# Two transformer stacks on one core: norms turned by token block, the next projection one block ahead, an eight-part weight ring

## The chip, the cores and the metric

One core of one Trainium2 chip runs the whole program. The metric is the device time of one execution in microseconds. TensorE (PE) multiplies, VectorE (DVE), ScalarE (ACT) and GpSimd (POOL) do the rest, and SyncE's queue (SPq) issues the weight loads. All engines run their own instruction streams in order and meet at semaphores.

## The reference

`x` has 256 tokens of 1024 features in float32. The first stack has four layers. Each layer has a mixer (sliding attention with sinks in layers 0 and 3, a gated linear recurrence in layer 1, latent attention in layer 2), cross attention over 256 memory tokens, and a gated feed-forward with a causal three-tap convolution over 2 x 2816 hidden features. After each of the three the tokens are normed:

```python
x = layer_norm(ALPHA * x + y, ln_g[i, 0], ln_b[i, 0])
x = layer_norm(ALPHA * x + memory_cross_attention(x, mem_k, mem_v, x_w_q[i], x_w_o[i]), ln_g[i, 1], ln_b[i, 1])
x = layer_norm(ALPHA * x + conv_glu_ffn(x, f_w_up[i], f_conv_w[i], f_conv_b[i], f_w_down[i]), ln_g[i, 2], ln_b[i, 2])
```

The second stack has two layers that add to the stream instead and norm by root mean square ahead of each part: an attention (with forget gates in layer 0, dilated in layer 1) joined with four heads over a second memory, then a feed-forward of the same size. A last root-mean-square norm gives the output.

## The kernel before

**Weights and precision.** Every matrix product with weights is done in three products of fp32r operands: each float32 is split into a rounded high part and the rest (`hi*hi + lo*hi + hi*lo`, `product`, lines 700 to 702). Weights come in 639 units of 128 x 1024 elements, 512 KB each. SyncE loads a unit into one of `RING` = 6 slots of `w_raw` (`unit_in`, line 525), waiting until the unit six earlier has been subtracted. ScalarE copies it into `w_hi` (`split`, line 1313) once PE has used the unit six earlier, and VectorE subtracts (`w_lo`, line 1728). Both do so at most `AHEAD` = 4 units ahead of the point that their program has reached (`Splitter.units`); `limit` caps this further at the end of a stage.

**Two forms of a projection.** In *feature form* a unit holds 128 output features, the weights are the stationary operand and the 256 tokens move: 24 products of 256 columns. In *token form* the turned tokens `xt` are stationary and 512 weight columns move: 12 products of 512 columns for a unit of two of the eight feature tiles, both token blocks. Feature form gives features on partitions (what a score needs), token form gives tokens on partitions.

**A stage boundary.** `out_finish` (line 1097) makes the second 512 columns of the mixer's or cross attention's output, all eight tiles of token block 0, then of block 1. VectorE adds the stream and takes statistics per block (`norm_part`, lines 2052 to 2058), GpSimd adds epsilon (L2264) and raises to -1/2 (L2266), VectorE scales in two passes (`norm_apply`, lines 2071 and 2074). PE then turns the 128 x 128 tiles of both blocks into banks 4 to 7, two tiles with both blocks to a bank (`turn_blocks`, L768). ScalarE copies each bank to `xt_hi` (L1353) and VectorE subtracts for `xt_lo` (L1743). Since a bank holds both blocks, nothing can be copied before block 1 is turned. The next stage's projection in feature form needs both blocks too. `seed_sums` (L1129) clears four banks with products of zeros for the feed-forward's down sums. The feed-forward (`feed_forward`, line 1132) does one tile of 128 hidden features at a time: two up units, the convolution on ScalarE (L1621) and VectorE (L2143), silu, product, split, and two tiles later one down unit (L1161).

**Order.** Each engine writes its whole program in stages: `program` calls the same steps on all five, and `attend` lays attention groups over one another, with `fill` giving PE projection or output units between groups. Nothing is reordered later.

## Time and profile before

| | us |
|---|---|
| median of 3 runs | 2255.78 (2255.22 to 2257.04) |
| the profiled execution | 2255.68 |
| its span | 2254.4 |
| PE / DVE / ACT / POOL busy | 2100.3 / 1539.6 / 1178.4 / 91.9 |

The clock granted to PE is 0.969 of full speed on average. Times inside the trace are microseconds from the start of the span. A line number names the instruction in the kernel before; `x12` means twelve instructions merged; brackets at the end give how long the engine was idle before and whose result ended that.

### The profile page before, as it was taken

How to read it: one execution, taken by the hardware profiler on the slowest of the kernel's cores; microseconds unless marked ns; L12 is line 12 of the kernel's file. 1: busy time of each engine (PE TensorE's matmuls, PEld its weight loads, DVE VectorE, ACT ScalarE, POOL GpSimd, SP SyncE). 2: the span in 40 equal slices, each digit the busy share in tenths (PEclk: the TensorE clock that was granted, in tenths of full speed). 3: DMA queues.
4: the chain of work that ended last, by engine and by line, in shares of the span. 5: the costliest groups of instructions: out<-in, count | busy, mean ns of one | idle time of the engine just before them, and what ended most of it. 6: DMA issues, size and time to landing. Idle time of an engine off the chain costs nothing.

```text
span 2254.4 us, 34080 instructions
## 1 busy us (share of the span) xinstructions
PE 2100.3 (93%) x13749; PEld 1909.1 (85%) x13749; DVE 1539.6 (68%) x2655; ACT 1178.4 (52%) x2027; POOL 91.9 (4%) x160
## 2 busy tenths in 40 slices
PE   7889999888999989899989999998998999999998
PEld 7778899787799978889977778997977999778997
DVE  4674777786677676577777757777465766666776
ACT  4453555484365555445545535554455555465554
POOL 3000000000000010000000000001000000000000
PEclk9999999998999999999999999999899999999999
DMA  8424666455366554456644437664624665424662
GB/s 279 149 76 136 180 189 189 129 168 168 111 198 179 179 157 121 132 167 186 181 159 134 126 100 222 181 184 126 179 66 140 196 195 179 154 93 136 191 194 87
DMA packets 436205, 356.24 MB, mean 158 GB/s; under 512 B 15858, under 2 KB 381686, under 8 KB 436048
## 3 DMA queue, kind: packets, MB, share of 16 engines
q1 hardware_dynamic: 429296, 332.49, 48.6%
q0 software_dynamic: 6752, 21.57, 2.9%
q8 instruction: 109, 1.79, 0.3%
q14 instruction: 48, 0.39, 0.1%
HBM read 352.97 MB, written 1.05 MB: 157 GB/s over the span
## 4 chain that ended last, share of the span: by engine, by line
PE 83%; DVE 9%; ACT 4%; issue 1%; POOL 1%; DMA 1%; SPq 0%; DVEq 0%; ACTq 0%
PE psum L700 20%; PE psum L702 20%; PE psum L701 20%; PE psum L1161 14%; PE psum L1057 3%; DVE w_lo L1728 1%; PE psum L1043 1%; PE psum L987 1%; DVE xt_lo L1743 1%; DVE x_tok L2074 1%; PE psum L826 1%; DMA tok<-in_mem_dram 1%; ACT w_hi L1313 1%; DVE n_tok L2052 1%; DVE small L2055 1%
## 5 line engine op out<-in xcount | busy, mean ns | idle before, releaser
L1728 DVE TENSOR_TENSOR w_lo<-w_raw,w_hi 128x1024 fp32r<-128x1024 f32 x639 | 752.3, 1223 | 158.8 <-ACT w_hi L1313 157.0
L700 PE MATMUL psum<-xt_hi,w_hi 128*128 128x256 f32 x2744 | 791.6, 288 | 23.1 <-DVE w_lo L1728 15.5
L701 PE MATMUL psum<-xt_lo,w_hi 128*128 128x256 f32 x2744 | 787.2, 287 | 0.0
L702 PE MATMUL psum<-xt_hi,w_lo 128*128 128x256 f32 x2744 | 786.7, 287 | 0.0
L1313 ACT CAST w_hi<-w_raw 128x1024 fp32r<-128x1024 f32 x639 | 646.9, 1048 | 84.5 <-PE psum L702 61.4
L700 PEld LDWEIGHTS psum<-xt_hi,w_hi 128*128 128x128 f32 x2744 | 537.8, 196 | 31.3 <-DVE xt_lo L1743 8.9
L701 PEld LDWEIGHTS psum<-xt_lo,w_hi 128*128 128x128 f32 x2744 | 537.8, 196 | 4.7
L702 PEld LDWEIGHTS psum<-xt_hi,w_lo 128*128 128x128 f32 x2744 | 537.1, 196 | 0.0
L2143 DVE SCALAR_TENSOR_TENSOR qt<-psum,par,qt 128x255 f32<-128x255 f32 (+1 forms) x528 | 217.9, 475 | 163.1 <-ACT qt L1621 162.9
L700 PE MATMUL psum<-w_hi,xt_hi 128*128 128x512 f32 (+4 forms) x700 | 261.8, 374 | 23.8 <-DVE xt_lo L1743 22.5
L702 PE MATMUL psum<-w_hi,xt_lo 128*128 128x512 f32 (+4 forms) x700 | 255.4, 365 | 0.0
L701 PE MATMUL psum<-w_lo,xt_hi 128*128 128x512 f32 (+4 forms) x700 | 255.2, 365 | 0.0
L1621 ACT ACTIVATE qt<-psum,par 128x256 f32<-128x256 f32 x264 | 134.5, 560 | 210.6 <-PE psum L702 210.6
L1161 PE MATMUL psum<-w_hi,hid_hi 128*128 128x512 f32 x528 | 207.8, 394 | 4.8 <-DVE hid_lo L2155 4.8
L1161 PE MATMUL psum<-w_lo,hid_hi 128*128 128x512 f32 x528 | 207.0, 392 | 0.0
L1161 PE MATMUL psum<-w_hi,hid_lo 128*128 128x512 f32 x528 | 205.6, 389 | 0.0
L700 PEld LDWEIGHTS psum<-w_hi,xt_hi 128*128 128x128 f32 x700 | 137.3, 196 | 48.5 <-issue 15.2
L702 PEld LDWEIGHTS psum<-w_hi,xt_lo 128*128 128x128 f32 x700 | 136.9, 196 | 19.9
L701 PEld LDWEIGHTS psum<-w_lo,xt_hi 128*128 128x128 f32 x700 | 137.4, 196 | 17.9
L1626 ACT ACTIVATE kt<-qt 128x256 f32<-128x256 f32 x132 | 55.1, 418 | 181.8 <-DVE qt L2143 181.7
L1353 ACT CAST xt_hi<-psum 128x512 fp32r<-128x512 f32 x78 | 40.9, 591 | 185.5 <-PE psum L768 185.5
L1743 DVE TENSOR_TENSOR xt_lo<-psum,xt_hi 128x512 fp32r<-128x512 f32 (+1 forms) x130 | 75.8, 617 | 67.8 <-ACT xt_hi L1539 39.2
(216 smaller groups left out, 1907.1 us busy)
## 6 DMA issues: line engine op xcount, KB each, us to landing
w_raw<-in_f_w_up_dram SPq DMA_DIRECT2D x176, 512.0 KB, 4.9
w_raw<-in_f_w_down_dram SPq DMA_DIRECT2D x88, 512.0 KB, 5.1
w_raw<-in_w_up_dram SPq DMA_DIRECT2D x88, 512.0 KB, 4.9
w_raw<-in_w_down_dram SPq DMA_DIRECT2D x44, 512.0 KB, 5.0
w_raw<-in_x_w_q_dram SPq DMA_DIRECT2D x32, 512.0 KB, 4.5
w_raw<-in_x_w_o_dram SPq DMA_DIRECT2D x32, 512.0 KB, 4.7
w_raw<-in_a_w_qkv_dram SPq DMA_DIRECT2D x24, 512.0 KB, 4.4
w_raw<-in_w_in_fox_dram SPq DMA_DIRECT2D x20, 512.0 KB, 4.7
```

The costliest lines, as they stand in the source:

```text
L700: self.eng.matmul(out, stat[0], mov[0], start=first, stop=False)
L701: self.eng.matmul(out, stat[0], mov[1], start=False, stop=False)
L702: return self.eng.matmul(out, stat[1], mov[0], start=False, stop=last)
L1057: ins = self.eng.matmul(m.psum[p0:p0 + wide, k, slot * SEQ + q0:(slot + 1) * SEQ], vals(c), m.pt[:, group.g % 2, i, cols], start=c == 0, s ...
L1161: ins = self.eng.matmul(m.psum[:, b + 2 * c, :], stat[x], unit[y][:, 0, cs], start=False, stop=last and x == 1, skip_group_check=True)
L1313: self.up(self.eng.copy(self.m.hi[:, s, :], self.m.raw[:, s, :]), "w_hi", u)
L1353: self.up(self.eng.copy(dst[0][:, j:j + nt, :], self.m.pair(4 + j // 2)[:, 0:nt, :]), "x_hi", self.tag, after, j)
L1621: ins = self.eng.activation(m.qt[:, 2 * s + half, :], out[half], ACT.Identity, scale=col((TAPS - 1) * 2 * FT + half * FT + q), bias=col(TA ...
L1626: self.up(self.eng.activation(m.kt[:, s, :], m.qt[:, 2 * s + silu_half, :], ACT.Silu), "silu", self.tag, q)
L1728: self.up(self.eng.tensor_tensor(self.m.lo[:, s, :], self.m.raw[:, s, :], self.m.hi[:, s, :].bitcast(F32), ALU.subtract), "w_lo", u)
L1743: n = self.up(self.eng.tensor_tensor(dst, src, hi.bitcast(F32), ALU.subtract), "ready", (tag, what), j)
L2143: ins = self.eng.scalar_tensor_tensor(cv[:, d:SEQ], out[half][:, 0:SEQ - d], col((TAPS - 1 - d) * 2 * FT + half * FT + q), cv[:, d:SEQ], A ...
```

## The change

- `RING` becomes 8 for the split parts `w_hi`, `w_lo`, and a new `RAW` = 4 is the number of raw slots. The freed memory also takes in `swap`, which now lies in the second half of `n_tok`'s block 1, and `zeros` goes away.
- `turn_half` turns four tiles of one token block into one bank (banks 4, 5 for block 0 and 0, 2 for block 1 at norms), and `split_half` copies and subtracts that bank alone. `operand` waits for the block that it reads.
- `out_finish` turns the first half of block 0 ahead of the last unit of block 1's products, the second half behind it, and leaves block 1's two turns in `rest`.
- `project_blocks` begins the next stage in token form: block 0 through four units, with the turns of `rest` behind its third and fourth unit, then block 1 through the same four. It makes the sliding queries' first half (now ahead of the keys), the latent keys, the first 512 of 1024 queries of cross attention and the first four feature tiles of the feed-forward. For the last two the tokens are copied to `n_tok` (`keep_first`) and turned to features by PE (`cross_queries`, `up_tile` for q below 2). The recurrence turns block 1 at once (`turn_now`).
- Cross attention's third and fourth query pair change places: the third stands around the turns, the fourth in step 0 of the attention.
- The norm's epsilon is added on VectorE (in `norm_part`, and in `rms_factor` by one instruction), and GpSimd is left with the power. Where the mean of squares comes from ScalarE, both operations stay on GpSimd.
- The down sums start with `start=True` at the first down unit instead of on zeros.
- The order on VectorE is changed: block 0 is scaled ahead of block 1's part, also at the end of a feed-forward.

The diff, cut:

```diff
+RAW = 4
+RING = 8
...
+def turn_bank(key, b, h):
+    return (4, 5, 6, 7)[2 * b + h] if key[0] == "start" or key[1] == "mem" else (4, 5, 0, 2)[2 * b + h]
...
-        s, k, n = u % RING, src.shape[1], src.shape[-1]
-        if u >= RING:
-            self.wait_ge("w_lo", u - RING)
+        s, k, n = u % RAW, src.shape[1], src.shape[-1]
+        if u >= RAW:
+            self.wait_ge("w_lo", u - RAW)
...
+        halves = w.rearrange("(k p) (h n) -> p k h n", p=P, h=2)
+        for j in range(0, KT, 2):
+            self.unit_in(halves[:, j:j + 2, :, 0:2 * P])
+        for m in range(2, FT + 2):
             if m < FT:
                 for half in range(2):
                     c = (half * FT + m) * P
                     self.unit_in(up[:, :, c:c + P])
-            if m >= 2:
-                self.unit_in(down[:, m - 2:m - 1, :])
+            self.unit_in(down[:, m - 2:m - 1, :])
...
+    def token_products(self, k, n, b, u, unit):
+        hi, lo = unit
+        kn = hi.shape[1]
+        for i in range(kn):
+            j = u * kn + i
+            ins = self.product(self.m.psum[:, k, 0:n], self.operand(j, slice(b * P, (b + 1) * P)),
+                               (hi[:, i, :], lo[:, i, :]), j == 0, j == KT - 1)
+        return ins
+    def project_blocks(self, what, ks, n, by="kept"):
+        units = []
+        for k in ks:
+            self.claim(k)
+        for u in range(KT // 2):
+            units.append(self.take(2, n))
+            ins = self.token_products(ks[0], n, 0, u, units[u])
+            if u == KT // 2 - 1:
+                self.up(ins, "made", self.tag, what, 0)
+            if u >= KT // 2 - 2 and self.rest:
+                self.rest.pop(0)()
+        for u, unit in enumerate(units):
+            ins = self.token_products(ks[1], n, 1, u, unit)
+            self.used(ins, "made", self.tag, what)
+        self.call("w_used", self.made["w_used"], "made", self.tag, what, 1)
+        for b, k in enumerate(ks):
+            self.free[k] = (by, self.tag, what, b)
+    def turn_half(self, key, b, h):
+        src = self.m.x_tok if key[1] == "norm" or key[0] == "first" else self.m.n_tok if key[1] == "applied" else self.m.tok
+        k = turn_bank(key, b, h)
+        if key[1] is not None:
+            self.wait_ge("normed", *key, b, h)
+        self.claim(k)
+        for a in range(HALF):
+            j = h * HALF + a
+            ins = self.eng.transpose(self.m.quad(k)[:, a, :], src[:, b, j * P:(j + 1) * P], self.m.ident[:])
+        self.up(ins, "turned", key, b, h)
+        self.free[k] = ("ready", key, "bank", b, h)
...
+    def turn_rest(self, key):
+        self.rest = [lambda: self.turn_half(key, 1, 0), lambda: self.turn_half(key, 1, 1)]
+        self.x = key
+    def turn_now(self):
+        while self.rest:
+            self.rest.pop(0)()
...
+    def cross_queries(self):
+        m = self.m
+        for j in range(2):
+            k = (4, 6)[j]
+            self.claim(k)
+            for b in range(TB):
+                self.wait_ge("kept", self.tag, "first", b)
+                for a in range(2):
+                    c = (2 * j + a) * P
+                    ins = self.eng.transpose(m.pair(k)[:, a, b * P:(b + 1) * P], m.n_tok[:, b, c:c + P], m.ident[:])
+            self.up(ins, "made", self.tag, "q", j)
+            self.free[k] = ("kept", self.tag, "q", j)
...
-    def out_finish(self, part):
+    def out_finish(self, part, scale, key):
 
         for b in range(TB):
             self.claim(b + 2)
-        units = [self.take(2, BANK) for _ in range(KT // 2)]
-        for b in range(TB):
-            for k in range(KT):
-                hi, lo = units[k // 2]
+        units = []
+        def products(b, j):
+            hi, lo = units[j]
+            for k in (2 * j, 2 * j + 1):
                 ins = self.product(self.m.psum[:, b + 2, :], self.out_tile(k, slice(b * P, (b + 1) * P)),
                                    (hi[:, k % 2, :], lo[:, k % 2, :]), k == 0, k == KT - 1)
-                if b == TB - 1 and k % 2 == 1:
-                    self.used(ins, "summed", self.tag, 1, 1)
-            if b == 0:
-                self.up(ins, "summed", self.tag, 0, 1)
+            return ins
+        for j in range(KT // 2):
+            units.append(self.take(2, BANK))
+            ins = products(0, j)
+        self.up(ins, "summed", self.tag, 0, 1)
+        for j in range(KT // 2):
+            if j == KT // 2 - 1:
+                self.turn_half(key, 0, 0)
+            self.used(products(1, j), "summed", self.tag, 1, 1)
         self.summed()
+        self.turn_half(key, 0, 1)
+        self.turn_rest(key)
...
+                if q >= 2:
+                    self.used(self.feature_out(out, self.take(KT, P)), "made", self.tag, q)
+                    continue
+                for b in range(TB):
+                    self.wait_ge("kept", self.tag, "first", b)
+                    c = (2 * half + q) * P
+                    ins = self.eng.transpose(out[:, b * P:(b + 1) * P], m.n_tok[:, b, c:c + P], m.ident[:])
+                if half == 1:
+                    self.up(ins, "made", self.tag, q)
+            self.free[k] = ("conv", self.tag, q)
...
+    def keep_first(self):
+        for b in range(TB):
+            self.units(2)
+            self.wait_ge("made", self.tag, "first", b)
+            self.keep([(self.m.n_tok[:, b, 0:BANK], self.m.psum[:, 6 + b, :])], "first", b)
...
+        part(0, 1)
+        scale(0)
+        self.split_half(key, 0, 0)
+        part(1, 1)
+        self.split_half(key, 0, 1)
+        scale(1)
+        for h in range(2):
+            self.split_half(key, 1, h)
+    def sums_to(self, part, scale, key):
+        for c in range(2):
+            part(0, c)
+        scale(0)
+        if key is not None:
+            self.split_half(key, 0, 0)
+        for c in range(2):
+            part(1, c)
+        if key is not None:
+            self.split_half(key, 0, 1)
+        scale(1)
+        if key is not None:
+            for h in range(2):
+                self.split_half(key, 1, h)
...
+            self.after(self.step(self.eng.bn_aggr(m.norm[:, 2 * b:2 * b + 2], stats[:, b, :])))
+            var = m.norm[:, 2 * b + 1:2 * b + 2]
+            self.up(self.eng.tensor_scalar(var, var, LN_EPS, None, ALU.add), "var", self.tag, b)
...
+        self.up(self.eng.scalar_tensor_tensor(part[0], part[0], RMS_EPS, part[1], ALU.add, ALU.add),
+                "var", self.tag, "x", b)
...
+    def power(self, r, mean, *which):
+        self.up(self.eng.tensor_tensor(r, mean, self.m.neg_half[:, 0:r.shape[1]], ALU.pow), "rstd", *which)
+    def power_of_squares(self, r, mean, *which):
+        self.wait_ge("squared", *which)
+        self.up(self.eng.tensor_scalar(r, mean, RMS_EPS, None, ALU.add), "pool", *which)
         self.wait_ge("pool", *which)
-        self.up(self.eng.tensor_tensor(r, r, self.m.neg_half[:, 0:r.shape[1]], ALU.pow), "rstd", *which)
+        self.power(r, r, *which)
```


## Rows read from the trace of the kernel before

**Rows 1.** The page, section 1: busy time, share and instructions of PE.
```profile
PE 2100.3 (93%) x13749; PEld 1909.1 (85%) x13749; DVE 1539.6 (68%) x2655; ACT 1178.4 (52%) x2027; POOL 91.9 (4%) x160
```
**Rows 2.** The view of waits, PE: us in total, times, longest us.
```profile
PE psum L768 <- DVE x_tok L2074: 47.9, 28, 3.5
PE psum L700 <- DVE xt_lo L1743: 29.5, 23, 8.9
```
**Rows 3.** Stretches: length, busy time per engine, PEclk, DMA share, GB/s.
```profile
157.64:164.08 6.44, 2.64 (x17) 2.00 (x16) 5.51 (x10) 1.11 (x3) 1.87 (x3) 0.85 0.00 0
164.08:168.92 4.84, 4.84 (x24) 4.84 (x23) 4.49 (x6) 4.82 (x6) 0.65 (x2) 0.50 0.62 223
229.80:236.75 6.95, 4.46 (x22) 2.90 (x20) 5.91 (x10) 1.63 (x4) 2.38 (x4) 0.79 0.00 1
426.62:437.81 11.19, 3.73 (x17) 2.54 (x17) 10.07 (x17) 1.11 (x3) 2.65 (x5) 0.73 0.04 14
1282.17:1284.90 2.73, 2.73 (x14) 2.73 (x14) 2.58 (x4) 2.73 (x5) 0.71 (x2) 0.50 0.65 170
```
**Rows 4.** The chain that ended last, first down products of two tiles in ffn0.
```profile
255.99 2.75 PE psum L1161 x12
264.49 2.75 PE psum L1161 x12
```
**Rows 5.** Timeline of the boundary mix0 to cross0: start, us, engine, line.
```profile
149.61 2.34 DVE L1728 TENSOR_TENSOR w_lo<-w_raw,w_hi 128x1024 fp32r<-128x1024 f32 x2
152.40 0.69 DVE L2052 SCALAR_TENSOR_TENSOR n_tok<-x_tok,psum 128x512 f32<-128x512 f32 x1 [0.45 <-PE psum L702]
153.85 0.21 DVE L2058 BATCH_NORM_AGGREGATE norm<-small 128x2 f32<-128x12 f32 x1
154.09 0.75 DVE L2071 SCALAR_TENSOR_TENSOR n_tok<-n_tok,norm,gain_row 128x512 f32<-128x512 f32 x1
154.15 0.77 POOL L2264 TENSOR_SCALAR norm<-norm 128x1 f32<-128x1 f32 x1 [124.56 <-DVE norm L2058]
155.01 0.57 POOL L2266 TENSOR_TENSOR norm<-norm,neg_half 128x1 f32<-128x1 f32 x1
157.06 0.75 DVE L2074 SCALAR_TENSOR_TENSOR x_tok<-n_tok,norm,bias_row 128x512 f32<-128x512 f32 x1
157.64 1.03 PE L768 MATMUL psum<-ident,x_tok 128*128 128x128 f32 x8
```
**Rows 6.** Timeline behind ffn0, GpSimd.
```profile
427.52 0.22 POOL L2264 TENSOR_SCALAR norm<-norm 128x1 f32<-128x1 f32 x1 [190.66 <-DVE norm L2058]
```
**Rows 7.** Timeline, PE: two waits, in ffn3 and ahead of second0.
```profile
1365.10 0.58 PE L700 MATMUL psum<-xt_hi,w_hi 128*128 128x256 f32 x1 [3.86 <-DVE w_lo L1728]
1570.75 0.66 PE L768 MATMUL psum<-ident,n_tok 128*128 128x128 f32 x2 [5.84 <-ACT mem_kt L1319]
```
**Rows 8.** Timeline, ScalarE: copies of turned keys and queries in mix3.
```profile
1201.85 2.60 ACT L1319 COPY kt<-psum 64x256 f32<-64x256 f32 x8 [4.83 <-PE psum L784]
1208.52 1.11 ACT L1321 ACTIVATE qt<-psum 128x512 f32<-128x512 f32 x2
```
**Rows 9.** A steady feed-forward: a load's issue, the casts (timeline), landings of 260 to 400.
```profile
304.44 0.37 SPq L525 DMA_DIRECT2D w_raw<-in_f_w_up_dram  x1
310.61 3.14 ACT L1313 CAST w_hi<-w_raw 128x1024 fp32r<-128x1024 f32 x3
DMA to landing us min/median/max: 3.4/5.2/7.2
```
**Rows 10.** Stretches behind two waits of PE, columns as in rows 3.
```profile
483.70:488.00 4.30, 4.30 (x36) 4.30 (x37) 3.35 (x3) 4.25 (x10) 1.37 (x1) 1.00 0.68 235
1228.14:1232.00 3.86, 3.86 (x14) 2.66 (x16) 2.26 (x13) 1.96 (x9) 0.00 (x0) 0.50 0.01 2
```
**Rows 11.** Timeline, PE: these two waits.
```profile
483.70 0.36 PE L700 MATMUL psum<-xt_hi,w_hi 128*128 128x256 f32 x1 [2.31 <-DVE w_lo L1728]
1228.14 1.23 PE L826 MATMUL psum<-kt,qt 128*128 128x128 f32 x3 [3.07 <-DVE stat L1991]
```

More of the change, by code:

```diff
@@ L761, in turn_blocks @@
             for j in range(tiles):
                 k = 4 + j // 2
-                if after is not None and j % 4 == 0:
-                    self.wait_ge("normed", self.tag, after, b, j // 4)
                 if j % 2 == 0 and b == 0:
@@ L890, in latent_start @@
                 self.turn_latent()
[L891 removed]
+            unit = self.take(2, C_QR)
             for b in range(TB):
[L893 to L896 removed]
+                ins = self.token_products(ks[b], C_QR, b, u, unit)
             self.used(ins, "made", self.tag, "cq")
@@ L1160, in down_part @@
             for x, y in ((0, 0), (0, 1), (1, 0)):
-                ins = self.eng.matmul(m.psum[:, b + 2 * c, :], stat[x], unit[y][:, 0, cs], start=False,
-                                      stop=last and x == 1, skip_group_check=True)
+                ins = self.eng.matmul(m.psum[:, b + 2 * c, :], stat[x], unit[y][:, 0, cs],
+                                      start=first and x == y == 0, stop=last and x == 1)
             return ins
+        self.project_blocks("first", (6, 7), BANK)
         for q in range(FT):
@@ L1570, in sum_unit, with out_finish @@
             self.units()
-    def out_finish(self, part):
+    def out_finish(self, part, scale, key):
         self.limit = self.unit + RING - 1
@@ L1638, in feed_forward, with sums_to @@
         self.limit = None
-    def sums_to(self, part):
+    def sums_to(self, part, scale, key):
         for b in range(TB):
@@ L1743, in low, with split_banks @@
         n = self.up(self.eng.tensor_tensor(dst, src, hi.bitcast(F32), ALU.subtract), "ready", (tag, what), j)
-        for a in range(1, nt):
+        for a in range(nt):
             self.call("ready", n, "ready", (tag, what), j + a)
+            for b in range(TB):
+                self.call("ready", n, "ready", (tag, what), j + a, b)
         self.call("ready", n, "ready", tag, what, j)
-    def split_banks(self, after, dst, tiles=KT):
+    def split_banks(self, after, dst, tiles):
         hi, lo = dst
@@ L1755, in split_banks, with split_half, split_turned @@
         self.call("ready", self.made["ready"], "ready", (self.tag, after), "hid")
+    def split_half(self, key, b, h):
+        hi, lo = (x[:, h * HALF:(h + 1) * HALF, b * P:(b + 1) * P] for x in self.m.xt)
+        self.wait_ge("x_hi", key, b, h)
+        n = self.up(self.eng.tensor_tensor(lo, self.m.quad(turn_bank(key, b, h)), hi.bitcast(F32), ALU.subtract),
+                    "ready", key, "bank", b, h)
+        for j in range(h * HALF, (h + 1) * HALF):
+            self.call("ready", n, "ready", key, j, b)
+    def split_turned(self, key):
+        for b in range(TB):
+            for h in range(2):
+                self.split_half(key, b, h)
+    norm_to_features = split_turned
     def start(self):
         self.eng = self.nc.vector
-        self.n_read = None
         self.e_read = [None, None]
-        self.step(self.eng.memset(self.m.zeros[:].bitcast(F32), 0.0), "zeros")
     def memory_keys_values(self):
-        self.split_banks(None, self.m.xt)
+        self.split_turned(("start", None))
         self.units(KT + KT)
@@ L2026, in sum_unit, with out_finish @@
             self.units()
-    def out_finish(self, part):
+    def out_finish(self, part, scale, key):
         self.limit = self.unit + RING - 1
@@ L2115, in add_part @@
         self.up(self.eng.tensor_tensor(h, h, m.psum[:, b + 2 * c, :], ALU.add), "added", self.tag, b, c)
-        if c == 1:
-            self.rms_factor(b)
-    def norm_to_features(self):
-        self.rms_apply(1)
-        for b in range(TB):
-            for c in range(2):
-                self.counts[("normed", self.tag, "norm", b, c)] = self.counts[("normed", self.factor, "applied", b, c)]
-        self.n_read = ("turned", self.tag, "norm", KT - 2)
-        self.split_banks("norm", self.m.xt)
     def feed_forward(self, params, silu_half):
@@ L2233, in memory_queries @@
         self.units(2)
-    def end(self):
-        self.rms_apply(1)
 class Pool(Engine):
@@ L2300, in stream_power, with sums_to @@
         m = self.m
-        self.power(m.norm[:, 20 + b:21 + b], m.norm[:, 16 + 2 * b:17 + 2 * b], RMS_EPS, "var", self.tag, "x", b)
-    def out_finish(self, part):
+        self.wait_ge("var", self.tag, "x", b)
+        self.power(m.norm[:, 20 + b:21 + b], m.norm[:, 16 + 2 * b:17 + 2 * b], self.tag, "x", b)
+    def sums_to(self, part, scale, key):
         for b in range(TB):
             part(b, 1)
-    def sums_to(self, part):
-        for b in range(TB):
-            for c in range(2):
-                part(b, c)
+    out_finish = sums_to
     def sliding_start(self, j):
```

340 lines of the change are left out of this document (148 added, 192 removed).

## The prediction

> **What bounds the kernel now.** I read the page's busy times first: PE is busy 2100.3 us of 2254.4 [rows 1]. So a change counts only through PE's idle time, its number of columns or its clock. Next I asked what PE waited for [rows 2]. The largest entry is the turning of the normed tokens (L768, 47.9 us), then the low halves of the turned tokens (L700 on L1743, 29.5 us). Both lie mostly at the stage boundaries. Stretches cut there [rows 3] show 6.44 us without a product between the output products and the next projection (157.64 to 164.08), 6.95 after cross attention and 11.19 after the feed-forward. All twelve gaps together, read the same way, are about 125 us, the 16 turns of each among them. Behind the gap the granted clock is 0.50 (1.2 GHz) for 4.84 us; at the last boundary of that kind it is so for 2.73 us. Half of that is lost: 2.4 to 1.4 us, together some 20 us.
>
> Rates: one feed-forward tile repeats every 8.50 us, and its 12 products of 512 columns take 2.75 [rows 4], 0.227 us each; the other 48, of 256 columns, then take 0.120 each. Eight turns show 1.03 us, of which the last one's end is drain: 0.9.
>
> **The change, one boundary worked through (mix0 to cross0).** Before, block 0 is complete at 152.40, the last product ends at 157.64 where the turns begin (call it E), the next starts at 164.08 [rows 3, 5]. Afterwards:
>
> The ring of 8 lets VectorE subtract four units ahead of block 0's norm instead of two. They start at 149.61 and cost 1.17 us each [rows 5], so the norm starts at 154.3, 1.9 us late. Add and statistics take 1.45 us (152.40 to 153.85), the aggregate 0.24, the new epsilon step as much: L2071 starts at 156.2. The Pool operation that goes away looks like 0.77 us, but the same operation takes 0.22 at 427.52, where VectorE is not in L2071 [rows 6]. In rows 5 it ends just behind L2071. So what is on Pool beside L2071 ends behind it, and now that is the power itself. Its bounds are 0.57 (not held) and 1.4 (held through L2071's 0.75, then 0.09 and 0.57). I take 1.4, as the nearest row is held: L2074 at 157.7, first half of block 0 at 158.4, second at 159.9. Against the old order the chain from Z (block 0 summed) to its end is 5.6 us, before 5.4 (157.06 + 0.75 - 152.40): the epsilon step gains nothing.
>
> The Trainium skill, SBUF — State Buffer, section Who interferes with whom, says that a VectorE instruction with two SBUF inputs contends with a GpSimd instruction that reads SBUF, and the second to issue waits. By that rule the trace agrees (0.77 beside L2071, 0.22 beside L2052, which reads one operand from PSUM), and the power would be held as I took it; without it all eight attention boundaries would give 0.65 us more, 5 us in all.
>
> PE reaches the first turn after 18 of block 1's 24 products, 152.20 + 4.08 = 156.3, waits 2.1 us there, turns (0.45), does the six last products (1.36, to 160.3), turns again; the low half is ready by 160.5 behind scale(0). First product of cross0: 160.7, not 164.08, and without half clock. Block 0's 24 products (5.44) then cover block 1's norm: its statistics end at 162.5, turned values at 164.7 and 166.2, where PE arrives at 164.8 and 166.7; with 8 turns (0.9) and block 1 (5.44) the four units are done at 172.5, E + 14.9. Before, they were at 178.0, E + 20.4 (6.44 + 96 x 0.120 + half clock + the last drain). Gain 5.5. Back go 8 turns of the query tokens (0.9), covered for their copies by cross_query(2, 0), and 0.3 because step 1 of the attention has lost its fill. That is 4.2 at cross0, and up to 1 us less where the old half clock was shorter: 3.65 mean, four times, **14.6**.
>
> **The others.** Cross to feed-forward: old 6.95 + 11.52 + 1.35 = 19.8; new 14.9 + 0.9 of turns + 0.65 for the copy of block 1 that nothing covers = 16.5. Three times 3.3: **9.9**. The zero products (four, inside the 6.95) lay in a wait; removing them is nothing.
> The two feed-forwards with the second memory's norm stop at 1365.10 and, alike, at 1732.42 [rows 7], because the squares and the 2.48 us of L1916 stand ahead of the splits. Now keep_first stands behind them too. I get E + 22 for the work that was done at E + 26: **4.0** at ffn3, **2.5** at gated0, whose memory load is issued 2 us later.
> Feed-forward to mixer: VectorE is the bound (10.07 of 11.19 us busy). First products start 4.7 + 0.65 us behind E instead of 11.2, but stop again for block 0's second half. Latent **+2.4** (its normed compressed keys also wait for a row load), sliding3 **+1.0** (the sink load, issued behind the norm, holds the splits, and q0's rotation holds its turn by 1.6), recurrent **-1.6**, since it turns everything first and pays the 0.24, the 0.65 and part(1, 0) earlier.
> Sliding now turns the keys last. Eight key copies take 2.60 us, two query copies 1.11 [rows 8]: scores start 1.9 later. In sliding3 it is in the sum already; mix0 has no gain against it: **-1.9**.
> Second stack: at 1570.75 PE waited 5.84 us for a key copy in the bank to be turned into [rows 7]; banks 0 and 2 relieve half: **+2.5**. Then **+1.0** (second1), **+1.6** (gated1: old 5.9 + 11.5, no half clock). Tail: rms_apply(0) now ahead of part(1, *): **-0.4**.
>
> **Raw units, 6 to 4.** In a steady tile the three loads are issued from 304.44, 1.14 us apart, and the casts start at 310.61 [rows 9]. With 4 slots these are units S+1 to S+3, S+1 cast at 311.66: 7.2 us after issue; landings there are 3.4/5.2/7.2. So nothing in most tiles; bounds 0 and about 1 us in a tile whose casts come late, and ScalarE's idle of 1.78 in a tile absorbs that. I take 0. Block products in tokens need 0.17 us less per unit, which is in the 5.44s.
>
> Sum: 14.6 + 9.9 + 6.5 + 1.8 - 1.9 + 5.1 - 0.4 = **35.6 us**. The profiled execution took 2255.68 us (span 2254.4), the median is 2255.78; 2255.7 - 35.6 = **2220**.
>
> **Rivals.**
> A, more: Pool isn't held beside L2071 and the loads for the third and fourth early split don't delay anything, the 2.1 us wait shrinks to 0.6 at eleven boundaries: 12 to 16 us more, **2206**. For it: only tiny operands; against it, rows 5 and 6.
> B, half clock stays: the wait at the turn, a further wait behind it and turns between make the clock fall again. A wait of 2.31 us left it at 1.00, one of 3.07 was followed by 0.50 [rows 10, 11]; mine is 2.1, between nothing and 3. If it falls at most boundaries, 11 x 1.8 = 20 us come back: **2240**.
> C, slower: four raw slots become the bound in the 132 feed-forward tiles. One mechanism, at L525: a load is issued only when the unit four before is subtracted. It decides from 35.6 / 132 = 0.27 us a tile; at 0.5 us a tile, about what a landing of 7.2 plus a late cast leaves, 66 us are added: **2286**. Against: PE uses a unit a whole tile after its subtraction.
> D, the change doesn't do what it says: one VectorE does both blocks in order, so block 0's lead is eaten by the early splits, scale(0) and copies, and only retransposition remains: within a few us of before, **2253**. Against: VectorE is busy 5.51 of the 6.44 us, and block 1's part of it now lies under products.
>
> **Chances.** Forecast 0.60 (own range 2212 to 2230), A 0.13, B 0.17, C 0.06, D 0.04. About 0.2% (4.5 us) is what can be told from no change. Faster: forecast, A and B, 0.90 and a little of D, 0.91; same 0.03; slower 0.06. Range 2205 to 2243: all of the forecast, most of A and B; C, D and the tails of A and B are out.
>
> **What would show it.** Right: no stretch without products longer than 3 us between output products and next projection; waits at L768 for x_tok near 2 us a boundary, 25 us in all; Pool's power about 1.3 us beside L2071; clock 1.00 across attention boundaries; the recurrent gap not shorter; kt copies last ahead of the first scores in sliding. Wrong: ScalarE's w_hi waiting for w_raw loads inside the feed-forward, tiles of more than 8.50 us, 0.50 behind attention boundaries, or a gap in step 1 of cross attention above 1 us. More than 50 us gained would mean that I misread what the wait for block 0 costs.

## The result, and the profile after

The changed kernel takes 2240.1 us (2239.5 to 2242.1, 4 runs) against 2256.4 (2255.2 to 2257.6, 4 runs) on the same chip: a ratio of 0.9928, 95% interval 0.9914 to 0.9942. It is faster, inside my range, but the gain is 16.3 us where I forecast 35.6. The number lies on that of rival B, but not by B's mechanism, as the runs show. The time of the profiled span is 2239.0 us (2254.4 before).

First the page of the changed kernel, its busy times, to be set against [rows 1]:

```profile
PE 2085.5 (93%) x13325; PEld 1876.8 (84%) x13325; DVE 1544.3 (69%) x2678; ACT 1179.8 (53%) x2047; POOL 73.5 (3%) x126
```

PE is busy 14.8 us less, and that is nearly the whole 15.4 by which the span shrank. Its waits did not shrink: those of 0.3 us and more, added up over the trace, are 143.7 us before and 143.3 after. They moved. The waits of PE in the changed kernel (instruction, what it waited for, us in total, times, longest), to be set against [rows 2]:

```profile
PE psum L814 <- DVE x_tok L2195: 26.7, 16, 4.8
PE psum L720 <- DVE qt L2247: 18.4, 6, 5.6
PE psum L720 <- DVE xt_lo L1835: 17.2, 10, 7.4
PE psum L1221 <- ACT n_tok L1391: 12.1, 8, 5.7
PE psum L895 <- ACT kt L1391: 4.7, 2, 2.3
```

The first row is the old L768, down from 47.9 to 26.7 (I had written 25). The second and fourth did not exist before. L2247 is VectorE's convolution of a feed-forward tile, and a product at L720 waits for it six times, once in each feed-forward: 2.36 us four times, 5.60 and 3.32 us in ffn3 and gated0, where the second memory's norm stands in VectorE's queue ahead of it. L1221 turns the first tiles' products back to features.

To place the gain I cut each trace at VectorE's first addition of a stage's sums (L2052 and L2115 before, L2173 and L2231 after); a stage's length is the distance between two such starts, so it begins inside the boundary ahead of it. Two pairs of these rows as an example, first of the kernel before:

```profile
219.11 0.69 DVE L2052 SCALAR_TENSOR_TENSOR n_tok<-x_tok,psum 128x512 f32<-128x512 f32 x1 [1.69 <-PE psum L702]
424.46 0.68 DVE L2052 SCALAR_TENSOR_TENSOR n_tok<-x_tok,psum 128x512 f32<-128x512 f32 x1
```

and of the changed one:

```profile
216.38 0.69 DVE L2173 SCALAR_TENSOR_TENSOR n_tok<-x_tok,psum 128x512 f32<-128x512 f32 x1 [1.67 <-PE psum L722]
421.80 0.68 DVE L2173 SCALAR_TENSOR_TENSOR n_tok<-x_tok,psum 128x512 f32<-128x512 f32 x1
```

So the stage ffn0 took 205.35 us before and 205.42 after. All stages, in us, as the difference from the kernel before (negative is a gain), beside the forecast; e1, e3 and f1 are experiments below:

| stage | before | forecast | changed | e3 features | e1 four banks | f1 |
|---|---|---|---|---|---|---|
| cross0, 1, 2, 3 | 72.2, 71.9, 71.2, 71.3 | -3.65 each | -4.8, -4.6, -3.9, -3.9 | -4.8, -4.6, -3.8, -3.9 | -4.4, -4.6, -3.8, -3.6 | -4.8, -4.6, -3.8, -3.6 |
| ffn0, 1, 2 | 205.4, 205.1, 204.9 | -3.3 each | +0.1, +0.4, +1.6 | +1.9, +2.2, +2.4 | -4.4, -4.1, -3.9 | -4.1, -3.8, -3.6 |
| ffn3, gated0 | 217.8, 218.1 | -4.0, -2.5 | -0.9, +2.7 | -4.7, -0.7 | -6.2, -3.0 | -10.7, -11.3 |
| gated1 | 201.0 | -1.6 | +2.3 | +4.0 | -1.8 | -1.8 |
| mix1, 2, 3 | 98.6, 93.1, 96.0 | +1.6, -2.4, -1.0 | +1.6, -2.4, -0.6 | +2.1, -2.6, -2.4 | +2.0, +1.4, +0.1 | +1.8, -1.8, -1.3 |
| second0, 1 | 148.4, 120.7 | -2.5, -1.0 | -1.7, -3.2 | -1.8, -3.1 | -1.8, -3.1 | -3.3, -3.1 |

Not every stage can be read so finely. mix0 ended at 146.96, 149.07 and 151.34 in three executions of which the last two are of the same code up to there. Over the traces of all versions whose code doesn't differ there, mix2 and second0 spread over some 4 us, mix3 and ffn3 over about 2, and ffn2 took 206.5 us in the changed kernel and 204.1 in e4. Most of the others repeat to some 0.4 us. What can be read: the attention boundaries gained what was forecast and a little more, and all six feed-forwards fell short, by 3.4, 3.7, 4.9, 3.1, 5.2 and 3.9 us: 24 us together.

What happens at their head, in the timeline of the changed kernel at ffn0 (start, us, engine; in brackets the idle time before it and what ended it):

```profile
241.84 0.59 ACT L1391 COPY n_tok<-psum 128x512 f32<-128x512 f32 x1 [0.61 <-PE psum L722]
242.48 0.98 PE L1221 MATMUL psum<-ident,n_tok 128*128 128x128 f32 x7 [0.57 <-ACT n_tok L1391]
243.06 1.02 ACT L1713 ACTIVATE qt<-psum,par 128x256 f32<-128x256 f32 x2 [0.64 <-PE psum L1221]
244.12 1.65 DVE L2247 SCALAR_TENSOR_TENSOR qt<-psum,par,qt 128x255 f32<-128x255 f32 x4 [1.44 <-ACT qt L1713]
245.82 0.39 PE L720 MATMUL psum<-xt_hi,w_hi 128*128 128x256 f32 x1 [2.36 <-DVE qt L2247]
```

The product at 245.82 is the first of tile 2. up_tile claims bank[q % 2], and tile 2's bank 4 is tile 0's, which the convolution reads until 245.77. Before the change the two up units of tile 1 (48 x 0.120 = 5.8 us) stood between tile 0's products and this claim. The same convolution in the kernel before:

```profile
245.57 1.65 DVE L2143 SCALAR_TENSOR_TENSOR qt<-psum,par,qt 128x255 f32<-128x255 f32 x4 [2.69 <-ACT qt L1621]
```

It ended at 247.22, and tile 2's first product came at 250.07. Now tiles 0 and 1 together are eight turns, and the last seven of them take 0.98 us. Behind the wait the clock falls (columns: stretch, its length, busy time and count of PE, PEld, DVE, ACT, POOL, granted clock, DMA share, GB/s):

```profile
245.82:250.82 5.00, 5.00 (x29) 5.00 (x30) 3.35 (x8) 2.67 (x7) 0.00 (x0) 0.66 0.41 120
```

A clock of 0.66 over 5 us is a mean of the two levels, 1.2 and 2.4 GHz; 1.7 us are lost in it. In the attention boundary it stays up, where [rows 3] had 0.50 for 4.84 us, and the first turns wait 1.28 us behind mixers and 1.59 behind cross attention; over the 13 to 16 us from the first turn it is 1.00 at all eight. Windows of the changed kernel at mix0 to cross0, from the first turn:

```profile
159.83:162.50 2.67, 2.67 (x16) 2.32 (x17) 2.55 (x4) 0.74 (x2) 0.00 (x0) 1.00 0.72 191
162.50:173.00 10.50, 10.50 (x52) 8.68 (x51) 8.64 (x14) 5.29 (x8) 1.69 (x3) 1.00 0.29 106
```

### The profile page after: what moved, and what is told of

It is laid out like the page before. It is cut to its first block, busy times and chain, and to the rows that moved or that the text cites. A ratio compares the mean times of both kernels' runs of the same rounds, so it can differ in the third digit from the quotient of the medians.

```text
span 2239.0 us, 33115 instructions
## 1 busy us (share of the span) xinstructions
PE 2085.5 (93%) x13325; PEld 1876.8 (84%) x13325; DVE 1544.3 (69%) x2678; ACT 1179.8 (53%) x2047; POOL 73.5 (3%) x126
## 3 DMA queue, kind: packets, MB, share of 16 engines
q8 instruction: 105, 1.72, 0.3%
## 4 chain that ended last, share of the span: by engine, by line
PE 79%; DVE 14%; ACT 4%; DMA 2%; issue 1%; POOL 1%; SPq 0%; DVEq 0%; ACTq 0%
PE psum L720 18%; PE psum L722 18%; PE psum L721 18%; PE psum L1230 15%; DVE w_lo L1820 4%; PE psum L1125 3%; PE psum L1111 1%; DVE small L2176 1%; DVE n_tok L2173 1%; PE psum L814 1%; PE psum L895 1%; PE psum L1054 1%; DMA tok<-in_mem_dram 1%; DVE qt L2247 1%; DVE x_tok L2195 1%
## 5 line engine op out<-in xcount | busy, mean ns | idle before, releaser
L720 PE MATMUL psum<-xt_hi,w_hi 128*128 128x256 f32 x2424 | 696.1, 287 | 29.4 <-DVE qt L2247 18.4
L721 PE MATMUL psum<-xt_lo,w_hi 128*128 128x256 f32 x2424 | 693.6, 286 | 0.0
L722 PE MATMUL psum<-xt_hi,w_lo 128*128 128x256 f32 x2424 | 693.3, 286 | 0.0
L720 PEld LDWEIGHTS psum<-xt_hi,w_hi 128*128 128x128 f32 x2424 | 472.3, 195 | 37.5 <-DVE qt L2247 20.1
L721 PEld LDWEIGHTS psum<-xt_lo,w_hi 128*128 128x128 f32 x2424 | 472.3, 195 | 4.8
L722 PEld LDWEIGHTS psum<-xt_hi,w_lo 128*128 128x128 f32 x2424 | 472.3, 195 | 0.0
L720 PE MATMUL psum<-w_hi,xt_hi 128*128 128x512 f32 (+4 forms) x860 | 328.8, 382 | 24.1 <-DVE xt_lo L1835 17.2
L2247 DVE SCALAR_TENSOR_TENSOR qt<-psum,par,qt 128x255 f32<-128x255 f32 (+1 forms) x528 | 218.1, 476 | 170.0 <-ACT qt L1713 170.0
L722 PE MATMUL psum<-w_hi,xt_lo 128*128 128x512 f32 (+4 forms) x860 | 318.4, 370 | 0.0
L721 PE MATMUL psum<-w_lo,xt_hi 128*128 128x512 f32 (+4 forms) x860 | 318.3, 370 | 0.0
L720 PEld LDWEIGHTS psum<-w_hi,xt_hi 128*128 128x128 f32 x860 | 167.2, 194 | 54.1 <-issue 16.2
L1230 PEld LDWEIGHTS psum<-w_hi,hid_hi 128*128 128x128 f32 x528 | 99.7, 189 | 24.6 <-DVE hid_lo L2259 7.3
```

The lines of the kernel that those rows point to most:

```text
L720: self.eng.matmul(out, stat[0], mov[0], start=first, stop=False)
L721: self.eng.matmul(out, stat[0], mov[1], start=False, stop=False)
L722: return self.eng.matmul(out, stat[1], mov[0], start=False, stop=last)
L1230: ins = self.eng.matmul(m.psum[:, b + 2 * c, :], stat[x], unit[y][:, 0, cs], start=first and x == y == 0, stop=last and x == 1)
L2247: ins = self.eng.scalar_tensor_tensor(cv[:, d:SEQ], out[half][:, 0:SEQ - d], col((TAPS - 1 - d) * 2 * FT + half * FT + q), cv[:, d:SEQ], A ...
```

## The experiments

My theory after the two traces: the forecast's mechanism works at every boundary, but the token form of the feed-forward's first tiles has taken away what covered tile 0's convolution, and bank 4 is not free. Rivals: tile 0's chain bounds the first down product anyway; the clock takes the gain; the token form is worth the forecast and the loss is in the tiles (four raw units); VectorE's early splits hold the norm. Each ratio below is taken against the kernel before on the same chip (its medians there are 2257.6 to 2258.6 us), so ratios compare between experiments better than times do. In the cuts of code, `...` marks what is left out.

**e1, four banks.** Tile q uses a bank of four in turn, in the three engines:

```
-        bank = (4, 6)
+        bank = (4, 6, 5, 7)
...
-            k = bank[q % 2]
+            k = bank[q % 4]
...
```

> Changed kernel, feed-forward tiles rotate over banks 4, 6, 5, 7 instead of 4, 6. Bank theory: in the changed kernel the gain of the new norm is given back behind the 8 re-turns, where tile 2 claims bank 4 while tile 0's convolution still reads it (L720 on qt L2247: 2.36 us four times, 3.32 and 5.60 once, 18.4 in all) and where the granted clock then falls to 0.50 (another 1.5 to 2.4 us each). With a free bank both go: 18 + 6 x 1.5 = 27 us less than the changed kernel's 2240, so about 2213 to 2220. Chain theory: the wait only changes its name, since the first down product needs tile 0's hid anyway and the second unit of tile 3 is subtracted only behind tile 1's convolution; then the waits move to L1230 on hid_lo or to L720 on w_lo and less than 5 us are won: 2235 to 2240. Clock theory: the wait goes but the clock still falls behind the boundary, 18 us less minus the half clock that stays: 2222 to 2226.

Measured: 2215.7 us, ratio 0.9814 (0.980 to 0.9828). The bank theory gave 2213 to 2220. The same place in e1's timeline:

```profile
244.82 0.98 PE L1221 MATMUL psum<-ident,n_tok 128*128 128x128 f32 x7 [0.57 <-ACT n_tok L1391]
245.40 1.02 ACT L1713 ACTIVATE qt<-psum,par 128x256 f32<-128x256 f32 x2 [0.64 <-PE psum L1221]
245.56 0.36 PE L720 MATMUL psum<-xt_hi,w_hi 128*128 128x256 f32 x1
246.46 1.65 DVE L2247 SCALAR_TENSOR_TENSOR qt<-psum,par,qt 128x255 f32<-128x255 f32 x4 [1.44 <-ACT qt L1713]
```

Tile 2's first product now has no wait and starts 0.9 us ahead of the convolution, and the stretch behind it, in e1's windows, is at full clock:

```profile
245.56:250.56 5.00, 5.00 (x45) 5.00 (x44) 3.03 (x8) 3.89 (x7) 0.00 (x0) 1.00 0.93 284
```

45 products in 5 us against 29. The wait on qt is gone from e1's list and none took its place, which falsifies the chain theory; the clock went with the wait, so it was no cause of its own. The six feed-forwards gain 29.5 us between them against the changed kernel; some 7 us of it went back in this execution in mix0, mix2 and mix3, stages that don't repeat. This is the cause of the miss, shown.

**e2, tile 2's first unit ahead of the re-turns** (on top of e1), to cover the copy at L1391:

```
...
+        up_tile(2, (0,))
+        up_tile(0)
+        up_tile(1)
+        up_tile(2, (1,))
...
```

> As e1_four_banks, and tile 2's first up unit is multiplied ahead of the 8 re-turns, its second behind them, so that ScalarE's copy of the first products (L1391, 12.1 us of waits at L1221, up to 5.7) lies beneath 2.9 us of products. Bank theory with this cover: another 4 x 0.57 plus most of 2.0 and 2.9 of the 7.6 us of the two stages with a memory norm, so 5 to 8 us less than e1_four_banks. Rival: tile 0's chain (base, convolution, silu, product, split, some 6.5 us) starts 2.9 us later and the first down product waits for it: no gain over e1_four_banks, within 2 us, and a new wait of 1 to 3 us at L1230 on hid_lo in each of the six feed-forwards.

Measured: 2221.5 us, ratio 0.9841 (0.9828 to 0.9855), 6 us slower than e1. The rival's direction held, its place only in part. PE's waits in e2:

```profile
PE psum L720 <- DVE w_lo L1826: 20.7, 5, 8.4
PE psum L1231 <- DVE hid_lo L2265: 10.9, 12, 1.0
```

The down products wait longer than in e1 (10.9 us in all against 4.8), 1.01 us more in each of the six feed-forwards, as the rival said. The waits for the copy, 11.0 us in e1, are gone. But w_lo takes 20.7 us where e1 had 8.5, and the growth lies in the two feed-forwards with the second memory's norm alone: 4.8 us at ffn3 and 8.4 at gated0, against 1.4 and none. At ffn3 VectorE scales the memory's tokens and clears mem_kt (1334.15 to 1338.97) before it subtracts the units that PE now wants sooner. It was VectorE's queue that I should have looked at.

**e3, the feed-forward's tiles 0 and 1 in features again**, two units each, all else as in the changed kernel:

```
...
-        self.project_blocks("first", (6, 7), BANK)
+        self.turn_now()
...
```

> Changed kernel, but the feed-forward's tiles 0 and 1 are projected in features again as before (units of 8 x 128 rows, no copy, no re-turns, and all four halves of the norm turned before the first product); the norm by blocks, the token form in cross attention and all else stay. Theory (the token form gives the feed-forward nothing in this form, because it lays bare tile 0's convolution): within 5 us of the changed kernel, 2235 to 2245. Rival (the token form is worth the 3.3 to 4 us a stage that I forecast, and the loss is somewhere else, in the tiles themselves): 6 x 3.5 = 21 us slower than the changed kernel, about 2260.

Measured: 2241.4 us, ratio 0.9931 (0.9916 to 0.9946), no difference from the changed kernel: in the form in which it was put in, the token form gave the feed-forwards nothing in all. By the table it wins 0.8 to 1.9 us in each of the four feed-forwards without a memory norm, 6.3 together, and loses 3.8 and 3.4 in ffn3 and gated0; with the bank free (e1) the same form is 6.3 us better than features in ffn0.

**e4, epsilon back on Pool**, ahead of the power.

```
+            self.up(self.eng.tensor_scalar(r, self.m.norm[:, 2 * b + 1:2 * b + 2], LN_EPS, None, ALU.add),
+                    "pool", self.tag, "eps", b)
```

> Changed kernel with the epsilon step back on Pool ahead of the power; the turns and all else stay. My forecast's step: the epsilon step on VectorE gains nothing, as the power is held beside L2192 anyway: then 2240 within 2 us. Rival (no hold: the power alone is done 0.5 to 0.8 us sooner at each of the eleven norms, and the wait at the first turn, 1.3 to 1.6 us, shows it): this kernel is 5 to 8 us slower than the changed one, 2245 to 2248. In the trace: Pool's power beside L2192 about 1.1 us and the first turn's wait the same (first case), or a wait at L814 longer by 0.5 or more (second).

Measured: 2242.6 us, ratio 0.9931 (0.9919 to 0.9944): not to be told from the changed kernel. The cross stages are longer by 0.4 to 0.5 us each, 1.8 us in all, and the first turns wait 1.72 us at the attention boundaries, where the changed kernel has 1.28 and 1.59. So the step does cost something on Pool, but the rival's 5 to 8 us don't show. Pool in the changed kernel at cross0's norm, then beside it the same operation at mix0's:

```profile
225.44 0.75 DVE L2192 SCALAR_TENSOR_TENSOR n_tok<-n_tok,norm,gain_row 128x512 f32<-128x512 f32 x1
225.49 1.12 POOL L2365 TENSOR_TENSOR norm<-norm,neg_half 128x1 f32<-128x1 f32 x1 [56.74 <-DVE norm L2181]
...
158.13 0.78 DVE L2192 SCALAR_TENSOR_TENSOR n_tok<-n_tok,norm,gain_row 128x512 f32<-128x512 f32 x1
158.18 0.57 POOL L2365 TENSOR_TENSOR norm<-norm,neg_half 128x1 f32<-128x1 f32 x1 [128.93 <-DVE norm L2181]
```

The power is held to 1.12 us at block 0 of the four cross norms and takes 0.55 to 0.57 at block 0 of the other eight of the first stack, where L2192 takes 0.77 or 0.78 instead of 0.75. In e4 the added step of 0.78 is held at block 0 each time and the power behind it (0.57) never.

**f1, the second memory's norm behind tile 8** instead of ahead of tile 0 (on top of e1):

```
...
+            if q == 8 and self.memory is not None:
+                self.memory_norm_now(self.memory)
...
```

> On top of e1_four_banks: the second memory's norm on ScalarE and VectorE is issued behind tile 8 of the feed-forward instead of ahead of its first tile. Theory (queue order: in ffn3 and gated0 ScalarE's two squares stand ahead of the copy of the first products, and VectorE's L2023 ahead of its splits): the waits at L1221 of 2.04 in ffn3 and 4.45 and 2.04 in gated0 fall to 0.57 or less, the 1.41 at L720 on w_lo goes, and the half clock behind them (1.11 and 1.31 by my count) too: 8 to 11 us less than e1_four_banks, 2205 to 2208. Rival: 3.5 us of work in the middle of a tile stretches the tiles there, since ScalarE and VectorE lie ahead of PE by less than that: 3 to 5 us come back at L1230 on hid_lo or L720 on w_lo, so 2209 to 2213.

Measured: 2201.8 us, ratio 0.9748 (0.9733 to 0.9762), 14 us less than e1 and more than either theory gave. What I had not seen is in e1's timeline at gated0:

```profile
1698.56 1.06 ACT L1568 ACTIVATE e<-tok 128x1024 f32<-128x1024 f32 x1 [4.69 <-DMA tok<-in_mem_dram]
...
1702.53 0.57 ACT L1391 COPY n_tok<-psum 128x512 f32<-128x512 f32 x1
1703.16 0.33 PE L1221 MATMUL psum<-ident,n_tok 128*128 128x128 f32 x1 [4.45 <-ACT n_tok L1391]
```

ScalarE stood 4.69 us for the load of the memory itself, with the copy that PE needed queued behind. In f1 there is no such wait. The kernel before has it too: there ScalarE's first square at gated0 (L1477) waits 5.93 us for the same load.

**h1, the kernel before with that move alone:**

> The kernel before the change, with the second memory's norm alone issued behind tile 8 of the feed-forward. It tells how much of the 14 us that this brought on top of e1_four_banks belongs to the changed kernel's copy of the first products (a copy the kernel before doesn't have). If the copy queued behind the squares is what cost it: the kernel before wins only its two waits of 3.9 us on w_lo and a part of the half clock behind them, 5 to 8 us, 2248 to 2252. If the norm's place costs the same in any form: 12 to 14 us, 2243.

Measured: 2243.1 us, ratio 0.9935 (0.9922 to 0.9948). So the second answer: the norm's place cost the kernel before as much (6.5 us in ffn3 and 6.2 in gated0 by the cut above), and this one move is worth as much as the whole change.

**f3, two of the four early splits behind the first turned half** (on top of e1), and **g2, one of the four** (on top of f1; `+ 6` for `+ 5`):

```
+        self.limit = self.unit + 5
         self.units(KT // 2)
         self.limit = None
         part(0, 1)
         scale(0)
         self.split_half(key, 0, 0)
+        self.units(0, more=True)
```

> On top of e1_four_banks: at the attention boundaries VectorE subtracts two units ahead of block 0's norm as before the change, and the other two behind the first turned half of block 0. Theory (the four early splits delay block 0's norm): the norm starts up to 2.4 us earlier, PE's wait at the first turn (1.27 to 1.6 us at ten boundaries) falls to 0 to 0.3, 8 to 12 us less than e1_four_banks: 2204 to 2208. Rival (the two splits moved behind scale(0) are needed as soon): the next projection's third unit, or block 0's second turned half and block 1's part, come 2.4 us later, and waits of 0.5 to 2 us at L720 on w_lo or at L814 on x_tok take their place: 0 to 6 us gained or lost, 2210 to 2220.

> On top of f1_memory_norm_late: three units subtracted ahead of block 0's norm at the attention boundaries, one behind the first turned half (f3 had two and two, and was 5 us slower than e1_four_banks). If the order of VectorE is a trade that has its best point between, the first turn's wait falls from 1.3 to 1.6 us to about 0.3 and xt_lo comes 1.2 us later, where f3 paid 15.2 us at L720 on L1855 over some eight boundaries: within 3 us of f1_memory_norm_late, 2199 to 2205. If each split behind the turn costs what it saves in front or more: 2 to 4 us slower.

Measured: f3 2220.8 us, ratio 0.9833 (0.9816 to 0.985); g2 2198.5 us, ratio 0.9738 (0.9725 to 0.9752). f3's waits show the trade:

```profile
PE psum L720 <- DVE xt_lo L1855: 22.7, 15, 2.5
PE psum L814 <- DVE x_tok L2197: 15.4, 8, 4.7
```

L814 falls by 12 us and L1855 rises by 15; as a whole f3 and e1 overlap in their intervals. One unit behind looks like the better point: the cross stages are 0.4 to 0.7 us shorter than f1's and ffn0 to ffn3 0.8, though as a whole g2 and f1 overlap in their intervals. g2 is the fastest version: 2.6% under the kernel before, 1.9% under the changed one.

**f4, three raw units** (`RAW = 3`, on top of e1), and **j1, six raw units and a ring of seven** (on top of g2):

> On top of e1_four_banks: three raw units instead of four. It tells whether the raw slots bound the tiles (rival C of the prediction) and how far off they are. If four were just enough, three make ScalarE's cast wait for a landing of 5.4 us in every feed-forward tile: at 0.5 to 1.5 us a tile 66 to 200 us more, 2280 or above. If the loads have slack (a unit is used a whole tile after its subtraction), nothing in the tiles and 5 to 15 us at the stage heads: 2220 to 2230.

> On top of g2_three_splits_early: six raw units and a ring of seven parts, where the changed kernel has four and eight (the same memory); the eighth unit is cast and subtracted behind block 0's first turned half. It asks what four raw units cost. In the changed kernel ScalarE waits about 70 us for w_raw landings where the kernel before waited 12, and at mix0 the four early subtractions start at 154.0 and not at 149.6 as I forecast, because casts wait 0.9 and 1.6 us for landings. If that is on the path, six slots let them start 2 to 4 us sooner: each of the eight attention boundaries 0.5 to 1.5 us shorter, 4 to 12 us less, 2187 to 2195. Rival: the landings are hidden (VectorE waits for block 0's sums anyway), and the ring of seven holds one unit back at each projection in blocks: within 3 us or up to 10 us slower, 2196 to 2208.

Measured: f4 2318.8 us, ratio 1.0264 (1.0239 to 1.0289); j1 2200.2 us, ratio 0.974 (0.9726 to 0.9753). With three units a tile still takes 8.50 us, so both my pictures of f4 were wrong: the cost is as high as in the first and the place that of the second. Each cross stage is 5 us longer, each feed-forward 6.5 to 15, all at their heads, as f4's waits say:

```profile
PE psum L814 <- DVE x_tok L2195: 48.1, 17, 5.2
PE psum L1221 <- ACT n_tok L1391: 38.0, 7, 13.3
```

j1 does away with ScalarE's waits for landings (all w_raw rows together 69.8 us in the changed kernel, 13.1 in j1) and gains nothing. They were hidden at mix0 too, against what I wrote ahead of j1. VectorE's first addition and its early splits, in the kernel before (the splits are in [rows 5], at 149.61) and in the changed one:

```profile
146.96 0.69 DVE L2052 SCALAR_TENSOR_TENSOR n_tok<-x_tok,psum 128x512 f32<-128x512 f32 x1 [1.70 <-PE psum L702]
...
149.07 0.69 DVE L2173 SCALAR_TENSOR_TENSOR n_tok<-x_tok,psum 128x512 f32<-128x512 f32 x1 [1.70 <-PE psum L722]
151.72 4.62 DVE L1820 TENSOR_TENSOR w_lo<-w_raw,w_hi 128x1024 fp32r<-128x1024 f32 x4
```

The splits start 2.65 us behind the first addition in both, and in j1 as well (151.52 and 154.17), with no wait ahead of them; the whole boundary lies later. Four is enough, three is not: rival C was one slot away, at the stage heads and not in the tiles.

**f5 and g1, a filler for PE at the three feed-forward to mixer boundaries**, 24 products on top of e1, then 6 on top of f1:

```
...
+            for _ in range(FILL):
+                ins = self.eng.matmul(self.m.psum[:, 7, 0:SEQ], self.m.mem_v[:, 0, 0:P], self.m.mem_v[:, 0, 0:SEQ],
+                                      start=True, stop=True)
...
```

> On top of e1_four_banks: at the three feed-forward to mixer boundaries PE runs 24 products of 256 columns into a bank that nobody reads (about 2.7 us of extra work, not part of the computation) behind the last down product, where it otherwise waits 2.90 us for block 0's norm. Clock theory: the granted clock falls to 0.50 there because PE stands still, so with the filler it stays at 1.00 behind the first turns; the half clock's cost of 0.74 to 0.93 at ffn0 and ffn1 and 2.0 at ffn2 goes: 3 to 5 us less than e1_four_banks in these stages. Rival: the later wait of 4.83 us (mix1) and of 3.17 (mix2) make it fall anyway and the filler delays the first turn by up to 0.3 us: within 1 us of e1_four_banks.

> On top of f1_memory_norm_late: the filler of f5_fill_24 with 6 products instead of 24 (they took 10.4 us for 24, 0.43 us each, so 6 take 2.6 us, against a wait of 2.6 to 2.9 us; they are not part of the computation). Clock theory: at ffn0, ffn1 and ffn2 the granted clock stays at 1.00 over the first turns and first products, 0.7 to 2 us less each: 2 to 4 us less than f1_memory_norm_late, 2198 to 2200. Rival: the wait for block 1 (4.8 us in mix1) makes the clock fall there all the same and the others are too small: within 1.5 us of it.

Measured: f5 2237.6 us, ratio 0.9903 (0.9886 to 0.9919); g1 2200.6 us, ratio 0.9751 (0.9737 to 0.9765). f5 was mis-sized and doesn't tell what the clock is worth; its filler in the timeline:

```profile
422.18 10.52 PE L1201 MATMUL psum<-mem_v 128*128 128x256 f32 x48
```

24 products in 10.5 us, 7.6 more than the wait of 2.9 that they were to fill. The three mixer stages are 7.2, 4.0 and 5.3 us longer than e1's, most of the 22 us by which f5 is slower. With six the clock stays up at ffn2's boundary. The 8 us from its first turn, f1 and then g1:

```profile
1153.86:1161.86 8.00, 7.62 (x25) 5.82 (x26) 7.34 (x13) 1.17 (x2) 0.55 (x1) 0.62 0.01 2
```

```profile
1151.26:1159.26 8.00, 6.50 (x33) 4.77 (x33) 7.68 (x14) 1.23 (x3) 0.54 (x1) 1.00 0.00 0
```

At 0.62 PE is busy 7.62 us with 25 instructions, at 1.00 it is busy 6.50 with 33: it waits for VectorE instead. At ffn1's boundary the same stretch goes from 0.79 to 0.96, at ffn0's from 0.58 to 0.89. But there PE waits 5.14 us for block 1 next, and behind that wait g1 shows

```profile
431.76:437.00 5.24, 4.86 (x20) 4.09 (x21) 3.25 (x8) 3.19 (x5) 1.10 (x2) 0.50 0.41 122
```

as g1's rival said. The three mixers are 1.2, 0.7 and 0.6 us shorter; the last two are less than mix2 and mix3 spread by themselves, and the whole can't be told from f1. VectorE is busy 7.68 of the 8 us there, so a faster PE mostly waits.

## Why the prediction was wrong, step by step

- **What bounds the kernel, attention boundaries (14.6):** right. The four cross stages gain 17.2 us. Counted from the first addition, block 0's sums are added 1.7 us later than before, where I had put 1.9 for the two more splits. The first turn waits 1.28 us behind mixers, where I had 2.1, since the power isn't held there, and 1.59 behind cross attention, where it is.
- **"Cross to feed-forward ... Three times 3.3: 9.9", ffn3 4.0, gated0 2.5, gated1 1.6:** this is the step that failed. I worked out when block 0's and block 1's products are done and added "0.9 of turns + 0.65 for the copy", and took for granted that the work of tile 2 follows. I counted what the re-turns cost and not what the products they replace had covered. The bank of tile 0 was not in my list of resources, though L2247 reads it and the claim is in the code. In ffn0 the claim costs 2.36 us of waiting and 1.7 of half clock, against a shortfall of 3.4. Measured: -2.0, +0.9, -2.7 and -2.3 us of gain in the place of 9.9, 4.0, 2.5 and 1.6. With the bank freed the same terms are 12.4, 6.2, 3.0 and 1.8 (e1), so the rest of the boundary was worth at least what I had, and e1 ends at 2215.7, where I had 2220. My 9.9 also took 1.35 us of old half clock; the kernel before lost 2.0 at ffn0 (0.50 from 236.75 to 240.70), so that term was small by 0.6 there.
- **Mixers (latent +2.4, sliding3 +1.0, recurrent -1.6):** the numbers are 2.4, 0.6 and -1.6. Only the recurrent one repeats (1.5 to 2.1 us longer in the changed kernel, e1, e3, e4 and f1). For the other two the agreement may be luck: mix2 runs from 2.6 us shorter to 1.4 longer in the same five, mix3 from 2.4 shorter to 0.1 longer. The kt copies come last ahead of sliding's scores and PE waits 2.35 us for them. mix0 can't be read, so its -1.9 is neither shown nor refuted.
- **Second stack, second0 +2.5, second1 +1.0:** 1.7 and 3.2, and second0 took 145.0 us in f1 and 149.1 in g1, whose code is the same there, so its 1.7 can't be told from 2.5. At second0 PE still waits 5.14 us for a key copy (5.84 before): the bank turned first is 4, whose key copy stands in ScalarE's queue behind the last squares and two casts, so banks 0 and 2 relieved 0.7 us at most.
- **Epsilon gains nothing:** nearly. It is worth about 2 us (e4). The power takes 1.12 us at block 0 of four norms and 0.57 at eight, where I took 1.4 at all.
- **Raw units, 0:** right (j1), for a reason I had not tested: my argument was about tiles, and the edge is at the stage heads (f4).
- **Rival B (half clock stays, 2240):** the number without the mechanism. The clock was half behind the re-turns, and went when the wait went (e1). **Rival A** was in the right direction for the first turn: Pool was free beside L2192 at eight of twelve norms. **C and D** did not occur.

Still open: why the waits at mix1 (7.4 us at L720 for xt_lo, 8.9 before) and second0 stay, and how much a free bank 4 at second0 would bring; neither was tried. That a wait on one bank explains all 24 us rests on e1 alone, and e1 also frees banks deeper in the tiles; a steady tile takes 8.50 us in both, so nothing shows there. Nor is it known why mix2, mix3, ffn3 and second0 spread by 2 to 4 us from one execution to the next.

## What to carry to other kernels

When an edit makes a step shorter, list what that step was lying over: the next user of the same buffer now arrives sooner, and with two buffers in turn it finds the first still read. Give an operation that nothing needs soon (a norm of another input, and the load it waits for) a place in the queues behind the work that PE waits for; here that one move was worth as much as the redesign of the boundaries. And compare traces by the length of each stage: two executions of the same code agreed to 0.4 us in most stages, so a term of 3 us can be checked by itself there; some stages spread by 4 us, and which these are shows only when the same code is traced more than once.

## What the runs showed of the hardware

- Products of 128 x 128 by 256 columns whose operands are plain f32 took 0.44 us each (10.52 us for 24, in f5) and show as two records each; those with fp32r operands take 0.120.
- Waits and the granted clock: 1.28 and 1.59 us at attention boundaries left it at 1.00, a wait of 2.31 us did so too in the kernel before [rows 10, 11], and 2.36 us behind eight turns was followed by 0.66 over the next 5 us. Six plain f32 products (2.75 us) in a wait of 2.9 kept it at 1.00 over 8 us at ffn2's boundary, and at ffn0's it was 0.50 behind the next wait of 5.14 us.
- Pool's power of one column beside a VectorE operation with two SBUF operands took 1.12 us at four norms and 0.55 to 0.57 at eight, and started 0.04 or 0.05 us behind that operation at all twelve. The Trainium skill, SBUF — State Buffer, section Who interferes with whom, says that issue order decides who blocks. These rows don't bear that out if the start times stand for the issue order, which the trace itself doesn't show: VectorE starts first each time, and Pool is held at only four. Where Pool isn't held, L2192 takes 0.77 or 0.78 us and where it is, 0.75, so VectorE loses 0.03 us and not the whole of Pool's instruction.
